# Three passages of a fused decoder layer reordered at once: the last mLSTM head turned sooner, the feed-forward begun under the last memory outputs, a copy and the weight sums moved in the up stage

## Chip, cores and metric

One core of a Trainium2 chip runs the whole kernel. The metric is device time in microseconds (us) from launch to end; lower is better. PE is TensorE, PEld its weight loads, DVE VectorE, ACT ScalarE, POOL GpSimd, SP SyncE, which here only issues DMAs.

## What is computed

A hybrid decoder layer over 1024 positions and 1024 features, f32, batch 1:

```python
h = rmsnorm(x, g_mix)                       # 3360 projected columns: NSA attention and mLSTM heads
x = x + concat(nsa_heads, mlstm_heads) @ w_out          # "mixer output"
q, k, v = rmsnorm(x) @ w_mem_q, rmsnorm(mem) @ w_mem_k, rmsnorm(mem) @ w_mem_v
x = x + softmax(q k^T / 16) v @ w_mem_o                 # "memory outputs"
hf = rmsnorm(x, g_ffn)
a, b = split(causal_conv3(hf @ w_up))                   # "up stage", 2 x 2816 columns
x = x + (gelu(a) * b) @ w_down                          # "down stage"
out = rmsnorm(x, g_final)
```

## The kernel before

**Products.** Activations lie transposed: 128 features on the partitions, 1024 positions along the row; `k` counts the eight feature blocks (KT = 8), `c` the two halves of 512 positions. Every f32 factor is split into a rounded high part and the rest, `h_hi`/`h_lo` and `w_hi`/`w_lo`, and `product` issues three matmuls of 128x512 per block: high by high, low by high, high by low. A weight tile of 128 output columns is so 8 x 2 x 3 = 48 matmuls. They collect in the eight 512-wide banks of PSUM, the tensor `ps`.

**Weights.** SP loads tiles in program order into two raw slots. POOL splits each (`split_tile`: `w_hi` by a multiplication, L871, then `w_lo` by a subtraction, L874) into two slots that alternate. It may write a slot when PE has begun the tile after the one that used it; a `tag` on one matmul of each tile counts the semaphore `tile_started`. `weights_split` tells PE that a tile is ready.

**Order.** Each engine has its own instruction list, written by hand; engines meet only at counting semaphores. DVE and ACT take banks in the order in which PE fills them (`chunk_done`, `chunk_freed`). So an instruction that waits holds up everything behind it on its engine.

**Mixer output.** The first two of eight output tiles (`mixed(z, c, k0, k1)`, z the tile) are interleaved, since the last head's block k = 7 is late: PE turns that head by eight small transposes (`turn_head(MH - 1)`, L1069), DVE scales it (L2404), ACT makes its high part (L1784), DVE its low part (L2137 through `split_head`), and only then may the products on k = 7 run (`split_ready`). Tile 2's weights take tile 0's slot.

**Memory outputs and the start of the feed-forward.** The first two of eight output tiles are interleaved with the attention; a loop (`gemm_loop`) does the other six, tile by tile. DVE adds each tile to the residual `x_t` (L2544, `add_residual`), ACT squares it (L1792) and saves it to DRAM, DVE adds the squares into `acc` (L2149). After the last tile ACT makes 16 high pieces (`split_hi`, L1799) and DVE 16 low pieces (`split_low`, L2138) of `x_t` in `h_hi`/`h_lo`, each a block k of a half c, over the activations that the memory outputs read. The first up tile takes them piece by piece (`plain_tile(0, 0, each_piece)`); behind it PE sums `acc` over features (`token_sums`, L1080), from which the norm's scale comes.

**Up stage.** 22 pairs of tiles p. The first three (PLAIN = 3) are plain; from p = 3 on each pair is one Strassen-Winograd step of seven half-size products of 12 matmuls, in the order a11, s1, s2, a12, s4, a22, s3. ACT makes the high operands and copies two product banks out (`take`, L1933: `p1_sum`, for which a12 waits, and `p5_sum`, for which s4 waits); POOL makes the low operands and sums (L933, L939). At p = 3 ACT first copies the activation operand t3 into `h_hi` (two `t_high`, L1922). In spare places POOL adds pairs of down-projection tiles (`s_new`, L959, "weight sums"): `S_AT` lists for each of the 22 the step at which it is done, two a step in steps 4 to 8 and one a step in 9 to 20. Before each of them SP loads its two tiles, the first two when `t_split` reaches 8, that is when t3's low part is made.

## Time and profile before

| | us |
|---|---|
| median of 3 runs (lowest, highest) | 1771.0 (1769.8, 1777.15) |
| the profiled execution's own time | 1772.6 |
| its span, first to last instruction | 1770.9 |
| PE busy in the span | 1691.8 (96%) |
| DVE / POOL / ACT busy | 1230.1 / 875.5 / 730.0 |
| mean granted TensorE clock | 0.98 of full |

In the timeline a row is: start, duration, engine, line, operation, out<-in, count, and in brackets how long the engine stood idle before it and what ended that. Lines are those of the kernel before. A matmul's duration overlaps the next one's; what counts is the distance between starts.

### The profile page before, as it was taken

What the parts mean: (1) busy time and instruction counts of PE and PEld (TensorE: products, weight loads), DVE (VectorE), ACT (ScalarE), POOL (GpSimd) and SP (SyncE); (2) the same over time, 40 slices, a digit from 0 to 9 for tenths busy, and PEclk for the clock granted to TensorE, in tenths of its full rate; (3) what the DMA queues carried; (4) which work ended last, traced back from release to release, by engine and by line L of the source; (5) the groups of instructions that cost most, each with busy time, mean ns of one, the idle gap of its engine ahead of it and who ended that gap; (6) DMA issues with size and microseconds to landing.
All of it is one profiled execution on the core that took longest, in us unless ns stands there. A gap on an engine that the chain in (4) does not pass through costs nothing.

```text
span 1770.9 us, 23263 instructions
## 1 busy us (share of the span) xinstructions
PE 1691.8 (96%) x8496; PEld 1414.8 (80%) x8496; DVE 1230.1 (69%) x1654; ACT 730.0 (41%) x1367; POOL 875.5 (49%) x671
## 2 busy tenths in 40 slices
PE   7998899999999999899999998989999999999997
PEld 6886788877788888789888776877788888877886
DVE  6754678776777787346554535768887887789965
ACT  5104677876223224115322303434434444543444
POOL 3343344543423332230322443469978878689851
PEclk9998999999999999999999999999999999999999
DMA  5230010110110112224201142145444445685332
GB/s 193 78 120 17 25 37 25 37 37 13 48 48 25 60 48 108 84 95 158 81 25 36 40 151 83 39 140 185 164 139 139 147 136 170 218 314 179 120 130 95
DMA packets 80331, 176.47 MB, mean 100 GB/s; under 512 B 7836, under 2 KB 24412, under 8 KB 80096
## 3 DMA queue, kind: packets, MB, share of 16 engines
q1 hardware_dynamic: 67944, 135.71, 23.2%
q10 hardware_dynamic: 12280, 39.34, 5.9%
q8 instruction: 66, 1.08, 0.3%
q14 instruction: 41, 0.34, 0.1%
HBM read 136.21 MB, written 38.81 MB: 99 GB/s over the span
## 4 chain that ended last, share of the span: by engine, by line
PE 56%; DVE 16%; POOL 11%; ACT 8%; issue 7%; DMA 1%; ACTq 0%; SPq 0%; POOLq 0%; DVEq 0%
PE ps L1028 13%; PE ps L1031 13%; PE ps L1032 13%; DVE x_t L2693 4%; PE ps L1207 3%; ACT x_t L1964 2%; POOL sum_s L939 2%; PE ps L1284 2%; POOL w_lo L933 2%; PE ps L1178 2%; POOL w_lo L989 2%; DVE x_t L2722 2%; PE ps L1226 2%; PE ps L1227 1%; PE ps L1179 1%
## 5 line engine op out<-in xcount | busy, mean ns | idle before, releaser
L1028 PE MATMUL ps<-h_hi,w_hi 128*128 128x512 f32 x1108 | 440.4, 398 | 22.0 <-DVE h_lo L2138 6.0
L1031 PE MATMUL ps<-h_lo,w_hi 128*128 128x512 f32 x1108 | 436.1, 394 | 0.0
L1032 PE MATMUL ps<-h_hi,w_lo 128*128 128x512 f32 x1108 | 435.7, 393 | 0.0
L871 POOL TENSOR_TENSOR w_hi<-w_raw,ones 128x1024 fp32r<-128x1024 f32 x55 | 115.0, 2091 | 549.2 <-PE ps L1028 465.8
L1028 PEld LDWEIGHTS ps<-h_hi,w_hi 128*128 128x128 f32 x1108 | 210.8, 190 | 75.3 <-ACT p_sum L1933 8.4
L1032 PEld LDWEIGHTS ps<-h_hi,w_lo 128*128 128x128 f32 x1108 | 210.7, 190 | 44.7
L1031 PEld LDWEIGHTS ps<-h_lo,w_hi 128*128 128x128 f32 x1108 | 210.9, 190 | 41.8
L899 POOL TENSOR_SCALAR probs<-probs,nsa_inv,gate_sig 128x640 f32<-128x640 f32 (+7 forms) x128 | 100.3, 783 | 172.5 <-DVE nsa_inv L2341 172.5
L2693 DVE SCALAR_TENSOR_TENSOR x_t<-ps,par,x_t 128x1023 f32<-128x1023 f32 x84 | 107.7, 1282 | 79.7 <-ACT x_t L1964 78.2
L874 POOL TENSOR_TENSOR w_lo<-w_raw,w_hi 128x1024 fp32r<-128x1024 f32 x55 | 146.4, 2662 | 4.3
L2137 DVE TENSOR_TENSOR pt_lo<-ps,pt_hi 128x512 fp32r<-128x512 f32 (+1 forms) x148 | 101.8, 688 | 58.0 <-ACT pt_hi L1704 56.1
L1207 PE MATMUL ps<-ident,probs 128*128 128x128 f32 (+1 forms) x592 | 96.4, 288 | 12.2 <-POOL probs L899 6.6
L1704 ACT ACTIVATE pt_hi<-ps 128x512 fp32r<-128x512 f32 (+1 forms) x148 | 87.7, 596 | 45.8 <-PE ps L1207 44.9
L1684 ACT ACTIVATE probs<-ps,nsa_shift 128x640 f32<-128x640 f32 (+7 forms) x128 | 89.8, 702 | 38.5 <-DVE nsa_shift L2329 21.4
L2329 DVE TENSOR_REDUCE nsa_shift<-ps 128x1 f32<-128x640 f32 (+7 forms) x128 | 88.9, 698 | 16.1 <-PE ps L1187 11.1
L1207 PEld LDWEIGHTS ps<-ident,probs 128*128 128x128 f32 (+1 forms) x592 | 65.5, 141 | 25.3 <-DVE pt_lo L2137 11.1
L1178 PE MATMUL ps<-k_a,q_st 128*128 128x512 f32 (+3 forms) x192 | 71.3, 371 | 11.9 <-ACT probs L1684 7.3
L2544 DVE TENSOR_TENSOR x_t<-ps,x_t 128x1024 f32<-128x1024 f32 x16 | 19.5, 1224 | 85.0 <-PE ps L1032 84.9
L2137 DVE TENSOR_TENSOR z_lo<-h_part,z_hi 128x512 fp32r<-128x512 f32 x40 | 58.8, 1484 | 11.7 <-ACT z_hi L2011 11.7
L933 POOL TENSOR_TENSOR w_lo<-w_raw,w_hi 128x512 fp32r<-128x512 f32 x38 | 51.4, 1353 | 29.3 <-ACT w_hi L1951 29.3
L1179 PE MATMUL ps<-k_a,q_st 128*128 128x512 f32 (+3 forms) x192 | 65.6, 348 | 0.0
L1226 PE MATMUL ps<-pt_hi,v_hl 128*128 128x512 f32 x132 | 64.5, 489 | 0.0
(374 smaller groups left out, 4108.5 us busy)
## 6 DMA issues: line engine op xcount, KB each, us to landing
w_raw<-in_w_tiles SPq DMA_DIRECT2D x109, 512.0 KB, 3.4
w_raw<-in_w_tiles SPq DMA_DIRECT2D x55, 256.0 KB, 3.0
s_new<-in_w_tiles SPq DMA_DIRECT2D x44, 256.0 KB, 4.1
z_dram<-x_t ACTq DMA_DIRECT2D x21, 512.0 KB, 2.9
b<-z_dram SPq DMA_DIRECT2D x33, 256.0 KB, 3.9
q_st<-q_dram SPq DMA_DIRECT2D x64, 128.0 KB, 2.8
x_dram<-x_t ACTq DMA_DIRECT2D x14, 512.0 KB, 2.7
t_dram<-t_new ACTq DMA_DIRECT2D x22, 256.0 KB, 5.2
```

Source lines behind the costliest of these rows:

```text
L871: pool.tensor_tensor(w_hi[s][:, :], w_raw[s][:, :], ones[:, :].to_broadcast([P, KT * P]), ALU.mult).then_inc(w_hi_made.sem, w_hi_made.up())
L874: pool.tensor_tensor(w_lo[s][:, :], w_raw[s][:, :], w_hi[s][:, :].bitcast(FP32), ALU.subtract).then_inc(weights_split.sem, weights_split.up())
L899: ins = pool.tensor_scalar(row, row, nsa_inv[:, j % 8, br:br + 1], gate_sig[:, i, 3 * h + 1 + br:3 * h + 2 + br], ALU.mult, ALU.mult)
L1028: ins = mm(out_ap, whi, x_hi, start=first, stop=False)
L1031: mm(out_ap, whi, x_lo, start=False, stop=False)
L1032: return mm(out_ap, wlo, x_hi, start=False, stop=last)
L1178: mm(o, qa, k_a[br][:, g, at_key:at_key + m], start=True, stop=False)
L1207: last = transpose(ps[0:width, 4 + k % 2, hd * P:hd * P + P], probs[:, at_p:at_p + width], ident[:, :])
L1226: mm(o, v, pt_hi[k % 3][0:e, :], start=br == 0 and a == 0, stop=False)
L1684: ins = f(probs[:, P_AT[j]:P_AT[j] + n], flat[:, 0:n], ACT.Exp, bias=nsa_shift[:, j % 8, br:br + 1], accum_out=nsa_sums[:, j % 8, br:br + 1])
L2137: return tt(out_lo, src, hi.bitcast(FP32), ALU.subtract)
L2693: ins = stt(fc[p][i][:, k:SEQ], ps_flat[:, b:b + SEQ - k], conv_f[:, FTAPS - 1 - k, n:n + 1], fc[p][i][:, k:SEQ], ALU.mult, ALU.add)
```

## The change

Three passages change.

1. *Mixer output.* Block k = 7 of tile 0 moves ahead of tile 1's last blocks, the head is turned after the first 12 instead of the first 33 matmuls of tile 1, and the tag that frees tile 0's weight slot sits on the first matmul behind tile 0.
2. *Feed-forward begun under the last memory outputs.* The last two output tiles leave the loop and are interleaved by blocks over banks 4 to 7. `out_read` tells ACT when blocks 0 to 3, and then 4 to 6, have been read, so that pieces (`FRONT`) are written over them while PE still works. The squares of the last two residual blocks come behind the pieces. The first up tile's weights get places of their own (`first_hi`, `first_lo`), split ahead of time.
3. *Up stage.* ACT's two t3 copies move behind the `p1_sum` copy and a tap; the weight sums begin at step 5, two a step in steps 5 to 10 and one a step in 11 to 20.

Two semaphores for small early loads become one (`small_loaded`).

```diff
-S_AT = [p for p in range(PLAIN + 1, FT - 1) for _ in range(2 if p < PLAIN + 6 else 1)]
+S_AT = [p for p in range(PLAIN + 2, FT - 1) for _ in range(2 if p < PLAIN + 8 else 1)]
+FRONT = ([(c, k) for c in range(2) for k in range(4)] + [(0, 4), (0, 5), (0, 6), (0, 7)] + [(1, k) for k in range(4, KT)])
@@ POOL
-            split_pairs((F1 - FIRST_KV - 2 * KT) // 2 - KT // 2 - 1)
+            split_pairs(KT // 2 - 1)
+            pool.wait_ge(loaded[1].sem, loaded[1].next())
+            pool.tensor_tensor(first_hi[:, :], w_raw[1][:, :], ones[:, :].to_broadcast([P, KT * P]), ALU.mult).then_inc(
+                w_hi_made.sem, w_hi_made.up())
+            pool.wait_ge(w_hi_made.sem, w_hi_made.value())
+            pool.tensor_tensor(first_lo[:, :], w_raw[1][:, :], first_hi[:, :].bitcast(FP32), ALU.subtract).then_inc(
+                weights_split.sem, weights_split.up())
+            tile_started.add(1)
+            split_tile(0)
+            split_pairs((F1 - UP) // 2 - 1)
@@ PE, mixer output
-            for z in range(2):
-                first_two.append(next_weights())
-                for c in range(2):
-                    mixed(z, c, 0, 4)
-                for c in range(2):
-                    mixed(z, c, 4, KT - 1)
-                    if z == 1 and c == 0:
-                        turn_head(MH - 1)
-            for z in range(2):
-                for c in range(2):
-                    mixed(z, c, KT - 1, KT).then_inc(chunk_done.sem, chunk_done.up())
+            first_two.append(next_weights())
+            for k0, k1 in ((0, 4), (4, KT - 1)):
+                for c in range(2):
+                    mixed(0, c, k0, k1)
+            first_two.append(next_weights())
+            mixed(1, 0, 0, 4)
+            turn_head(MH - 1)
+            mixed(1, 1, 0, 4)
+            mixed(1, 0, 4, KT - 1)
+            for c in range(2):
+                mixed(0, c, KT - 1, KT).then_inc(chunk_done.sem, chunk_done.up())
+            mixed(1, 1, 4, KT - 1)
+            for c in range(2):
+                mixed(1, c, KT - 1, KT).then_inc(chunk_done.sem, chunk_done.up())
@@ PE, memory outputs
-            gemm_loop(KT // 2 - 1, 2, h_hi, h_lo)
-            freed_now()
+            gemm_loop(KT // 2 - 2, 2, h_hi, h_lo)
+            middle = chunk_done.n
+            ring.resize(4, 4)
...
+            for k0, k1 in ((0, 4), (4, KT - 1)):
+                for z in range(2):
+                    if not k0:
+                        last_two.append(next_weights())
+                    for c in range(2):
+                        ins = last_outputs(z, c, k0, k1)
+                ins.then_inc(out_read.sem, out_read.up())
+            for z in range(2):
+                for c in range(2):
+                    last_outputs(z, c, KT - 1, KT).then_inc(chunk_done.sem, chunk_done.up())
+            taken(middle)
...
-            plain_tile(0, 0, each_piece)
+            plain_tile(0, 0, front_piece, weights=(first_hi, first_lo))
+            h_ready.n = front_from + 2 * KT
+            freed_now()
@@ ACT, memory outputs
+            for n, (c, k) in enumerate(FRONT):
+                if n == 0:
+                    act.wait_ge(t("out_read").sem, 1)
+                elif k == 4 and c == 0:
+                    act.wait_ge(t("out_read").sem, 2)
+                elif k >= KT - 2 and c == 0:
+                    chunk_done.add(2)
+                    freed_now()
+                split_hi(x_t, c * KT + k, c * KT + k + 1, G_FFN)
+            square_and_save(KT - 2)
+            square_and_save(KT - 1)
@@ ACT, up stage
-                if p == PLAIN and PLAIN < FT:
-                    after_product(PLAIN - 1, 7)
-                    for name, part in T_SPLITS[6:]:
-                        t_high(name, part)
                 if PLAIN <= p < FT:
                     take(p, 1, p1_sum, 0, t("p1_taken"))
                 high_operand(p + 1, "a11")
...
                     first_tap(p - 1, 1)
+                if p == PLAIN:
+                    for name, part in T_SPLITS[6:]:
+                        t_high(name, part)
@@ DVE, memory outputs
+            for c, k in FRONT:
+                if c == 0 and k >= KT - 2:
+                    add_output(k)
+                dve.wait_ge(chunk_freed.sem, chunk_freed.value())
+                split_low(x_t, c * KT + k, c * KT + k + 1, G_FFN)
+            for u in range(2):
+                add_square(u)
```

DVE's list at the end of the memory outputs (`x_t<-ps,x_t` is a residual block, `acc<-acc,sq` its squares, `h_lo` a low piece), before:

```order
1064 L2544 TENSOR_TENSOR x_t<-ps,x_t 128x1024 [waits chunk_done,xh_loaded]
1065 L2544 TENSOR_TENSOR x_t<-ps,x_t 128x1024 [waits chunk_done,x_parked]
1066 L2149 TENSOR_TENSOR acc<-acc,sq_167 128x1024 [waits sq_used,sq_ready]
1067 L2149 TENSOR_TENSOR acc<-acc,sq_168 128x1024 [waits sq_used,sq_ready]
1068 L2138 SCALAR_TENSOR_TENSOR h_lo<-x_t,par,h_hi 128x512 [waits hi_ready,chunk_freed]
1069 L2138 SCALAR_TENSOR_TENSOR h_lo<-x_t,par,h_hi 128x512 [waits hi_ready] x15
```

and of the change:

```order
1064 L2195 SCALAR_TENSOR_TENSOR h_lo<-x_t,par,h_hi 128x512 [waits hi_ready,chunk_freed] x10
1065 L2601 TENSOR_TENSOR x_t<-ps,x_t 128x1024 [waits chunk_done,xh_loaded]
1066 L2195 SCALAR_TENSOR_TENSOR h_lo<-x_t,par,h_hi 128x512 [waits hi_ready,chunk_freed]
1067 L2601 TENSOR_TENSOR x_t<-ps,x_t 128x1024 [waits chunk_done,x_parked]
1068 L2195 SCALAR_TENSOR_TENSOR h_lo<-x_t,par,h_hi 128x512 [waits hi_ready,chunk_freed] x5
1069 L2206 TENSOR_TENSOR acc<-acc,sq_167 128x1024 [waits sq_used,sq_ready]
1070 L2206 TENSOR_TENSOR acc<-acc,sq_168 128x1024 [waits sq_used,sq_ready]
```

Ten pieces now stand ahead of the last two residual blocks, and the squares behind all sixteen.

ACT's list around p = 3 of the up stage (`w_hi<-sum_s` is the high part of s3, `h_hi<-x_t` the t3 copy, the first `p_sum` the take for a12, the second the take for s4), before:

```order
701 L1951 ACTIVATE w_hi_53<-sum_s_190 128x512 [waits sum_made]
702 L1922 ACTIVATE h_hi<-x_t 128x2x512 [waits t_made,prod_done]
703 L1922 ACTIVATE h_hi<-x_t 128x2x512 [waits t_made]
704 L1933 ACTIVATE p_sum<-ps 128x512 [waits prod_done]
705 L1951 ACTIVATE spare_hi_181<-w_raw_169 128x512 [waits w_loaded2,prod_done]
706 L1964 ACTIVATE x_t<-ps,par 128x1024 [waits up_ready,z_stored0]
707 L1933 ACTIVATE p_sum<-ps 128x512 [waits prod_done]
```

and of the change:

```order
706 L2009 ACTIVATE w_hi_53<-sum_s_190 128x512 [waits sum_made]
707 L1991 ACTIVATE p_sum<-ps 128x512 [waits prod_done]
708 L2009 ACTIVATE spare_hi_181<-w_raw_169 128x512 [waits w_loaded2,prod_done]
709 L2022 ACTIVATE x_t<-ps,par 128x1024 [waits up_ready,z_stored0]
710 L1980 ACTIVATE h_hi<-x_t 128x2x512 [waits t_made] x2
711 L1991 ACTIVATE p_sum<-ps 128x512 [waits prod_done]
```

The two copies have moved from ahead of the first take to directly ahead of the second.

POOL's list behind the loop that splits the memory output tiles (numbers behind names are buffers), of the change; before, the loop simply ran on over these tiles with `w_hi` and `w_lo`:

```order
219 L929 TENSOR_TENSOR first_hi<-w_raw_52,ones 128x1024 [waits w_loaded1]
220 L932 TENSOR_TENSOR first_lo<-w_raw_52,first_hi 128x1024 [waits w_hi_made]
221 L874 TENSOR_TENSOR w_hi_53<-w_raw_51,ones 128x1024 [waits tile_started,w_loaded0]
222 L877 TENSOR_TENSOR w_lo_55<-w_raw_51,w_hi_53 128x1024 [waits w_hi_made]
223 L285 UNCONDITIONAL_BRANCH
```

The first up tile's split no longer waits for PE to begin a tile; the second one's does, as before.

## Rows read from the trace of the kernel before

**Rows 1.** The page, busy time and instructions of each engine.

```profile
PE 1691.8 (96%) x8496; PEld 1414.8 (80%) x8496; DVE 1230.1 (69%) x1654; ACT 730.0 (41%) x1367; POOL 875.5 (49%) x671
```

**Rows 2.** Timeline of PE, first two mixer output tiles.

```profile
699.79 0.48 PE L1028 MATMUL ps<-h_hi,w_hi 128*128 128x512 f32 x1
...
716.94 1.03 PE L1069 MATMUL ps<-ident,h_mls 128*128 128x128 f32 x8
...
721.82 0.50 PE L1028 MATMUL ps<-h_hi,w_hi 128*128 128x512 f32 x1 [1.79 <-DVE h_lo L2137]
...
728.48 0.79 PE L1028 MATMUL ps<-h_hi,w_hi 128*128 128x512 f32 x1 [3.64 <-POOL w_lo L874]
```

**Rows 3.** Timeline of DVE, then POOL, same stretch.

```profile
708.91 1.23 DVE L2492 TENSOR_TENSOR h_mls<-u_conv,head_d 128x1024 f32<-128x1024 f32 x1
718.07 1.28 DVE L2404 SCALAR_TENSOR_TENSOR o_gate<-ps,par,o_gate 128x1024 f32<-128x1024 f32 x1 [7.93 <-PE ps L1069]
720.54 1.22 DVE L2137 TENSOR_TENSOR h_lo<-o_gate,h_hi 128x1024 fp32r<-128x1024 f32 x1 [1.19 <-ACT h_hi L1784]
...
723.79 1.89 POOL L871 TENSOR_TENSOR w_hi<-w_raw,ones 128x1024 fp32r<-128x1024 f32 x1 [18.98 <-PE ps L1028]
725.76 2.67 POOL L874 TENSOR_TENSOR w_lo<-w_raw,w_hi 128x1024 fp32r<-128x1024 f32 x1
```

**Rows 4.** Windows behind three idle times: from:to, length, busy (matmuls), clock ("PEclk" follows POOL).

```profile
1092.21:1096.56 4.35, 4.34 (x10) 3.46 (x11) 4.35 (x4) 4.35 (x8) 3.42 (x2) 0.51 0.00 0
728.40:734.90 6.50, 6.42 (x16) 5.03 (x17) 6.14 (x6) 2.11 (x2) 4.31 (x3) 0.52 0.25 81
1196.00:1199.00 3.00, 2.94 (x7) 2.39 (x8) 2.69 (x3) 0.85 (x3) 3.00 (x3) 0.52 0.82 210
```

**Rows 5.** Timeline of PE, last two memory output tiles to the token sums.

```profile
1065.66 0.39 PE L1028 MATMUL ps<-h_hi,w_hi 128*128 128x512 f32 x1
...
1092.21 0.77 PE L1028 MATMUL ps<-h_hi,w_hi 128*128 128x512 f32 x1 [4.63 <-DVE h_lo L2138]
...
1106.84 1.84 PE L1080 MATMUL ps<-ones,acc 128*128 128x1 f32 x16
```

**Rows 6.** Timeline of POOL, DVE and ACT, same stretch.

```profile
1068.11 3.26 POOL L874 TENSOR_TENSOR w_lo<-w_raw,w_hi 128x1024 fp32r<-128x1024 f32 x1
...
1087.72 1.22 DVE L2544 TENSOR_TENSOR x_t<-ps,x_t 128x1024 f32<-128x1024 f32 x1 [9.65 <-PE ps L1032]
1088.86 2.54 DVE L2149 TENSOR_TENSOR acc<-acc,sq 128x1024 f32<-128x1024 f32 x2
...
1089.94 9.90 ACT L1799 ACTIVATE h_hi<-x_t,par 128x512 fp32r<-128x512 f32 x16
```

**Rows 7.** Windows of DVE's `h_lo` pieces: from:to, length, busy (pieces), clock.

```profile
1093.00:1098.00 5.00, 5.00 (x3) 0.65 0.00 0
1098.00:1105.80 7.80, 7.77 (x12) 1.00 0.19 67
```

**Rows 8.** Timeline of ACT, PE and POOL, steps 3 and 4 of the up stage.

```profile
1173.78 1.99 ACT L1922 ACTIVATE h_hi<-x_t 128x1024 fp32r<-128x1024 f32 x2
...
1177.66 0.59 ACT L1933 ACTIVATE p_sum<-ps 128x512 f32<-128x512 f32 x1
...
1176.30 0.50 PE L1028 MATMUL ps<-h_hi,w_hi 128*128 128x512 f32 x1 [3.07 <-ACT p_sum L1933]
...
1196.06 0.77 PE L1028 MATMUL ps<-t_hi,spare_hi 128*128 128x512 f32 x1 [2.77 <-POOL spare_lo L933]
...
1201.02 0.50 PE L1028 MATMUL ps<-h_hi,w_hi 128*128 128x512 f32 x1 [0.63 <-ACT p_sum L1933]
...
1188.34 1.30 POOL L959 TENSOR_TENSOR s_new<-s_new,s_new 128x512 f32<-128x512 f32 x1 [5.26 <-DMA s_new<-in_w_tiles]
```

**Rows 9.** Windows: three steps of two weight sums, ten of one; columns as rows 4, POOL fifth.

```profile
1220.53:1279.01 58.48, 58.41 (x253) 46.88 (x253) 49.00 (x46) 24.73 (x37) 54.98 (x40) 1.00 0.48 166
1301.00:1491.50 190.50, 190.50 (x840) 157.13 (x840) 153.52 (x151) 82.43 (x120) 156.76 (x121) 1.00 0.45 149
```

More of the change, by code:

```diff
@@ L489, in build @@
         y_tok = [at(f"y_tok{i}", (32 + 4 * i) * KB, [P, D]) for i in range(TT)]
+        first_hi = at("first_hi", FREE + 96 * KB, [P, KT * P], FP32R)
+        first_lo = at("first_lo", FREE + 100 * KB, [P, KT * P], FP32R)
         part = lambda name, offset, dt=FP32: at(name, offset, [P, HALF], dt)
@@ L2647, in _, with add_output @@
             clear_sums(acc)
-            for n in range(0, KT, 2):
-                for k in (n, n + 1):
-                    if k >= PARK:
-                        back = (t("xh_loaded", 16), t("x_parked", 16))[k % 2]
-                        dve.wait_ge(back.sem, back.next())
-                    add_residual(k)
+            def add_output(k):
+                if k >= PARK:
+                    back = (t("xh_loaded", 16), t("x_parked", 16))[k % 2]
+                    dve.wait_ge(back.sem, back.next())
+                add_residual(k)
+            for n in range(0, KT - 2, 2):
+                add_output(n)
+                add_output(n + 1)
                 for u in range(2):
                     add_square(u)
-            dve.wait_ge(chunk_freed.sem, chunk_freed.value())
-            split_low(x_t, 0, 2 * KT, G_FFN)
+            ring.resize(4, 4)
+            for c, k in FRONT:
[5 more added lines that the diff above has]
+                add_square(u)
             columns_start(4)
```

48 lines of the change are left out of this document (31 added, 17 removed).

## The prediction

> **What bounds the kernel now.** I read the page's busy times first: PE is busy 1691.8 us of 1770.9 [rows 1], so a microsecond counts only if it takes idle or slow time from PE. Then PE's timeline around the three passages. In the mixer output PE stands idle 1.79 us for the last head's block and 3.64 us for a weight tile [rows 2]. Between memory outputs and feed-forward it is idle 4.63 us [rows 5]. In the up stage it waits 3.07, 2.77 and 0.63 us in steps 3 and 4 [rows 8]. Behind three of these idle times the granted clock is 0.51 or 0.52 of full, that is the 1.2 GHz level: 10, 16 and 7 matmuls [rows 4]. At full clock a matmul takes 190.50/840 = 0.2268 us [rows 9], so the slow stretches lose 4.35 - 2.27 = 2.1, 6.5 - 3.6 = 2.9 and 3.0 - 1.6 = 1.4 us.
>
> I make the sum against the profiled execution, 1770.9 us span and 1772.6 us time; that time lies 1.6 us over the median of the three runs, so a saving is taken off 1771.0.
>
> **Mixer output.** The products stay 84, only their order changes. From the start at 699.79, 54 matmuls (42 of tile 0, 12 of tile 1) end at 712.1; there the head is turned, where before it was at 716.94 [rows 2]. Its input is ready at 708.91 + 1.23 = 710.1 [rows 3], so 2.0 us of slack cover this. Before, the low part ended 721.76 - 716.94 = 4.8 us after the turn began [rows 3]; now that is 716.9. The turn costs PE 1.05 us (from 716.94 to 721.82 - 1.79 = 720.03, less 9 matmuls, 2.04), and 21 matmuls (4.8 us) behind it don't need the block: until 717.9. The 1.79 us wait goes, with 1.0 us to spare.
>
> The weight slot: the tag now fires after 6 more matmuls, at 719.3. Before it was the seventh of the last 12, at 723.3, and POOL began at 723.79 and ended 723.79 + 1.97 + 2.67 = 728.43 [rows 3]. Now it begins at 719.8 and ends at 724.4, or 725.0 if its `w_lo` takes the 3.26 us that one takes beside DVE's adds [rows 6]. PE is done with its 15 remaining matmuls at 722.7 and waits 1.7 us, not 3.64. Tile 2 begins at 724.4 instead of 728.48: 4.1 us. Whether the clock falls again adds 2.9 or nothing. The 1.79 us wait was followed by matmuls 0.23 us apart up to the next stop, the 3.64 us one by clock 0.52 [rows 2, 4]; 1.7 us is nearest to the first, so I take full clock: 7.0 us. Ends: 3.5 (slow again, long `w_lo`) and 8.3 (1.79 + 3.64 + 2.9, all gone).
>
> **Start of the feed-forward.** Call 1065.66, where the last two output tiles begin, T. The token sums begin at 1106.84 = T + 41.2 [rows 5]. Between them lie 96 + 48 matmuls, 32.7 us. So at most 8.5 us can go. What waits remain?
>
> First, the second tile's weights are wanted after 24 matmuls (T + 5.4) and not after 48. POOL's `w_lo` begun at 1068.11 ends at 1071.37 = T + 5.7 [rows 6]: a new wait of 0.3 us.
>
> Second, the pieces. Blocks 0 to 3 are read at T + 11.2; their 8 pieces cost ACT 9.90/16 = 0.62 us each [rows 6] and DVE 7.77/12 = 0.65 each [rows 7], and are through by T + 18, four microseconds ahead of PE. Blocks 4 to 6 are read at T + 19.7. Then in a row: ACT 0.6, DVE's pieces (0,4), (0,5) to T + 21.7, the residual block 6 (1.22 [rows 6]) to T + 22.9, ACT 0.8, piece (0,6) to T + 24.4, residual block 7 to 25.6, ACT 0.8, piece (0,7) to T + 27.1. PE ends the outputs at T + 22.1 and has 21 matmuls before block 7: T + 26.9. Alone this waits 0.2 us. But POOL splits the second up tile's weights just then, from PE's start at T + 22.1 on (two instructions, about 2.0 and 2.7 us [rows 3]), and beside such a split DVE got only 3 pieces into 5.00 us where it otherwise did 12 in 7.77 [rows 7]. So a piece gets in between POOL's two instructions, and (0,6) and (0,7) are each about half an instruction late: I take 1.2 us of wait. Then the second half needs no wait: its four late pieces come 0.65 to 1.2 us apart, while 12 matmuls on ready blocks (2.7 us) pass first. The squares follow at T + 31.5 and cost DVE 2.54 [rows 6]: T + 34.1. PE reaches the token sums at T + 32.7 + 0.3 + 1.2 = T + 34.2. Gain 41.2 - 34.2 = 7.0 us. The cover is thin: each microsecond by which DVE is later comes off. Ends: 8.2 (no wait but the first) and 4.8, if both pieces miss POOL's gap and stand behind a whole instruction each (3.4 us of wait). `first_hi`/`first_lo` cost nothing: POOL does them from T + 5.7 to about T + 10.4, 12 us before they are used.
>
> The Trainium skill, "SBUF — State Buffer", section "Who interferes with whom", says that a VectorE instruction with two SBUF inputs and a GpSimd one that reads SBUF can't run together, and that whoever starts first holds the port for the whole instruction. The rows above agree (3 pieces in 5.00 us beside POOL). By the rule alone, with POOL always first, this passage would give the 4.8 us; by the rows 7.0.
>
> **Up stage.** ACT is free at 1173.78, now takes `p1_sum` at once, and a12 begins at 1174.4 instead of 1176.30. But the two copies (1.99 us) now lie ahead of the second take, which ended at 1177.66 + 0.59 = 1178.25 before [rows 8] and ends there still. So s4 begins at 1178.3 after a new wait of 1.2 us; before it began 12 matmuls after 1176.30, at 1179.0. Of 1.9 us only 0.7 stay.
>
> In step 4 POOL's two sums are gone, and with them its 5.26 us wait for their load [rows 8], which came late because the load waits for t3's low part. POOL's next low part then comes over 4 us sooner, before PE asks for it. From s4 at 1178.3 to a12 of step 4 are 6 products, 72 matmuls, 16.3 us: 1194.6, plus 0.2 for the take. Before it was 1201.02 [rows 8]: 6.2 us. This contains the 2.77 us wait and the 1.4 us of slow matmuls.
>
> Against it: a step with two sums lasts 58.48/3 = 19.49 us, one with a single sum 84 x 0.2268 = 19.05 [rows 9]; POOL is busy 54.98 of 58.48 us in the former. Step 4's own two are off the path now, but steps 9 and 10 become double: 2 x 0.44 = 0.9 us back. Net 5.3 us. Ends: 3.3 (2.8 + 1.4 - 0.9, the takes gain nothing) and 7.9 (3.07 + 2.77 + 0.63 + 1.4, no double cost).
>
> The merged semaphore for small loads costs nothing: PE merely waits for one more load of the kernel's first microseconds, over 100 us old by then.
>
> **Sum.** 7.0 + 7.0 + 5.3 = 19.3 us; 1771.0 - 19.3 = 1751.7. The stages behind are PE-bound (190.50 busy of 190.50 [rows 9]), so what is gained stays.
>
> **Rivals.** (a) *Passages half delivered*: clock down behind the 1.7 us wait, pieces behind whole POOL instructions, the takes gaining nothing: 3.5 + 4.8 + 3.3 = 11.6 us, 1759. For it: the port rows; the clock fell after 2.77 and 3.64 us [rows 4, 8]. Against: three independent misfortunes.
> (b) *Given back at the next wait*: the head's low part comes 3.5 us beyond its slack, the squares keep PE from the token sums for as long, and the clock falls at both (2.9 and 2.1 us). The mixer then keeps 7.0 - 6.4 = 0.6 us, the feed-forward 7.0 - 5.6 = 1.4; with 5.3 that is 7.3 us: 1764. For: squares end 0.1 us before they are wanted. Against: nothing in DVE's list grew.
> (c) *Slower*: POOL stalls for the sums' loads in each double step, as at 1188.34, since the sums keep their loads behind the same gate and SP's list is reshuffled. One such stall costs 2.77 + 1.4 = 4.1 us; six of them 24.8, and 19.3 off: 1776.5. It decides from the fifth on. Against: in steps 5 to 8 before, POOL shows no such wait (three double steps are 54.98 of 58.48 busy [rows 9]).
> (d) *All waits go*: 24.4 us, 1747.
>
> **Chances.** Forecast 0.70 (its own range 1748 to 1756), (a) 0.13, (b) 0.08, (c) 0.04, (d) 0.05. The ends of the three terms sum to 11.6 and 24.4 us, so 1746.6 to 1759.4; I give 1747 to 1760. A measurement of this kernel tells 0.5%, some 9 us: faster is forecast, (a) and (d), 0.88; same (b), 0.08; slower (c), 0.04.
>
> **What would show it.** Mixer: turn near 712, no wait on `h_lo` behind it, a wait of 1.4 to 2.3 us on `w_lo`, clock 1.0 behind it. Feed-forward: token sums 34 to 35 us after the last two tiles begin, a wait near 0.3 us on the second tile's weights and one of 0.2 to 3.4 us before block 7 of the first half. Up stage: about 1.2 us between a12 and s4 of step 3, no stall of POOL on `s_new` in step 5, 19.5 us steps from 5 to 10 and 19.05 behind. The prediction is wrong if PE's waits in these places sum to over 8 us, or if a new slow stretch stands behind the 1.7 us wait.

## The result, and the profile after

| | before | after |
|---|---|---|
| median of 4 runs each, taken together | 1770.4 us | 1753.16 us |
| lowest to highest | 1768.93 to 1777.15 | 1752.93 to 1756.01 |
| span of the profiled execution | 1770.9 | 1751.2 |
| mean granted clock | 0.98 | 0.984 |

The ratio is 0.9898, with a 95% interval of 0.9879 to 0.9917: about 18 us faster, between 14.7 and 21.4. The whole interval lies beyond the 0.5% that the prediction named as the bound of a measurement, so this is faster. Predicted were 1751.7 us (1747 to 1760) and 19.3 us of gain.

The page of the changed kernel, busy times. PE's work is the same as in [rows 1], and it lost 5.8 us of busy time; fewer of its matmuls ran at the lower clock (mean granted clock 0.984 instead of 0.98):

```profile
PE 1686.0 (96%) x8496; PEld 1410.7 (81%) x8496; DVE 1231.1 (70%) x1654; ACT 730.7 (42%) x1367; POOL 880.8 (50%) x671
```

**Mixer output.** PE's timeline, changed kernel (start, duration; idle before it and what ended that in brackets), the rows that answer to [rows 2]:

```profile
702.25 0.48 PE L1040 MATMUL ps<-h_hi,w_hi 128*128 128x512 f32 x1
...
714.63 0.38 PE L1081 MATMUL ps<-ident,h_mls 128*128 128x128 f32 x2
...
726.82 0.50 PE L1040 MATMUL ps<-h_hi,w_hi 128*128 128x512 f32 x1 [1.62 <-POOL w_lo L877]
```

DVE and POOL in the same stretch, for [rows 3]:

```profile
715.76 1.28 DVE L2461 SCALAR_TENSOR_TENSOR o_gate<-ps,par,o_gate 128x1024 f32<-128x1024 f32 x1 [3.17 <-PE ps L1081]
718.24 1.23 DVE L2194 TENSOR_TENSOR h_lo<-o_gate,h_hi 128x1024 fp32r<-128x1024 f32 x1 [1.20 <-ACT h_hi L1830]
...
722.10 1.90 POOL L874 TENSOR_TENSOR w_hi<-w_raw,ones 128x1024 fp32r<-128x1024 f32 x1 [14.86 <-PE ps L1040]
724.08 2.69 POOL L877 TENSOR_TENSOR w_lo<-w_raw,w_hi 128x1024 fp32r<-128x1024 f32 x1
```

(The row of the turn shows the first two of its eight transposes.) The head is turned 12.4 us after the start instead of 17.2, no wait for its low part is left, and one of 1.62 us stands before tile 2. Tile 2 begins 24.57 us after the start (726.82 - 702.25) instead of 28.69.

**Start of the feed-forward.** PE's timeline, for [rows 5]:

```profile
1058.28 0.39 PE L1040 MATMUL ps<-h_hi,w_hi 128*128 128x512 f32 x1
...
1064.04 0.50 PE L1040 MATMUL ps<-h_hi,w_hi 128*128 128x512 f32 x1 [0.16 <-POOL w_lo L877]
...
1086.34 0.50 PE L1040 MATMUL ps<-h_hi,first_hi 128*128 128x512 f32 x1 [0.91 <-DVE h_lo L2195]
...
1092.59 1.84 PE L1092 MATMUL ps<-ones,acc 128*128 128x1 f32 x16
```

The last two output tiles begin at 1058.28, the token sums 34.3 us later instead of 41.2. DVE and POOL there, for [rows 6]:

```profile
1080.14 1.22 DVE L2601 TENSOR_TENSOR x_t<-ps,x_t 128x1024 f32<-128x1024 f32 x1
1082.22 1.26 DVE L2195 SCALAR_TENSOR_TENSOR h_lo<-x_t,par,h_hi 128x512 fp32r<-128x512 f32 x1 [0.86 <-ACT h_hi L1845]
1083.41 1.21 DVE L2601 TENSOR_TENSOR x_t<-ps,x_t 128x1024 f32<-128x1024 f32 x1
...
1088.86 2.54 DVE L2206 TENSOR_TENSOR acc<-acc,sq 128x1024 f32<-128x1024 f32 x2
...
1081.04 1.90 POOL L874 TENSOR_TENSOR w_hi<-w_raw,ones 128x1024 fp32r<-128x1024 f32 x1 [11.75 <-PE ps L1040]
1083.02 2.72 POOL L877 TENSOR_TENSOR w_lo<-w_raw,w_hi 128x1024 fp32r<-128x1024 f32 x1
```

The piece (0,6) at 1082.22 lasts 1.26 us, twice a piece's usual time. It begins while POOL's `w_hi` runs and ends 0.54 us after that has ended. The squares end at 1091.4, 1.2 us before the token sums.

**Up stage.** PE, then ACT, for [rows 8]:

```profile
1150.66 0.39 PE L1040 MATMUL ps<-h_hi,spare_hi 128*128 128x512 f32 x1
...
1160.16 0.50 PE L1040 MATMUL ps<-h_hi,w_hi 128*128 128x512 f32 x1 [1.18 <-ACT p_sum L1991]
...
1164.07 0.50 PE L1040 MATMUL ps<-h_hi,w_hi 128*128 128x512 f32 x1 [0.87 <-ACT p_sum L1991]
...
1180.93 0.50 PE L1040 MATMUL ps<-h_hi,w_hi 128*128 128x512 f32 x1 [0.25 <-ACT p_sum L1991]
...
1161.54 1.99 ACT L1980 ACTIVATE h_hi<-x_t 128x1024 fp32r<-128x1024 f32 x2
1163.43 0.59 ACT L1991 ACTIVATE p_sum<-ps 128x512 f32<-128x512 f32 x1
```

From a11 of step 3 to a12 of step 4 (1150.66 to 1180.93) PE takes 30.27 us instead of 36.11. The second wait is the one predicted behind the two copies.

The clock, in windows of the changed kernel (from:to, length, busy of PE, PEld, DVE, ACT, POOL, granted clock, DMA share, GB/s): behind tile 2's wait, behind the take for a12, and three double steps, for [rows 4, 9]:

```profile
726.80:733.30 6.50, 6.48 (x28) 5.36 (x29) 6.08 (x7) 2.13 (x2) 4.31 (x2) 1.00 0.31 94
...
1160.10:1163.10 3.00, 2.94 (x12) 2.17 (x12) 1.39 (x2) 3.00 (x5) 3.00 (x3) 1.00 0.34 98
1199.91:1258.40 58.49, 58.47 (x254) 46.79 (x253) 48.99 (x46) 24.73 (x37) 55.04 (x39) 1.00 0.51 176
```

Where the 19.7 us between the spans lie, by landmarks in PE's timeline:

| stretch | before | after | gain |
|---|---|---|---|
| start to the mixer output | 699.79 | 702.25 | -2.5 |
| to tile 2 | 28.69 | 24.57 | 4.1 |
| to the last two memory output tiles | 337.2 | 331.5 | 5.7 |
| to the token sums | 41.2 | 34.3 | 6.9 |
| to a11 of step 3 | 58.07 | 58.07 | 0 |
| to a12 of step 4 | 36.11 | 30.27 | 5.8 |
| to the down stage's first product (1538.07, 1518.84) | 337.05 | 337.91 | -0.9 |
| to the end | 232.8 | 232.4 | 0.5 |

### The profile page after: what moved, and what is told of

It reads as the page before. It is cut to its first block, busy times and chain, and to the rows that moved or that the text cites. A ratio compares the mean times of both kernels' runs of the same rounds, so it can differ in the third digit from the quotient of the medians.

```text
span 1751.2 us, 23264 instructions
## 1 busy us (share of the span) xinstructions
PE 1686.0 (96%) x8496; PEld 1410.7 (81%) x8496; DVE 1231.1 (70%) x1654; ACT 730.7 (42%) x1367; POOL 880.8 (50%) x671
## 4 chain that ended last, share of the span: by engine, by line
PE 54%; DVE 14%; POOL 13%; issue 9%; ACT 8%; DMA 1%; SPq 0%; ACTq 0%; POOLq 0%; DVEq 0%
PE ps L1040 13%; PE ps L1044 12%; PE ps L1043 12%; DVE x_t L2760 4%; PE ps L1219 3%; POOL sum_s L951 2%; ACT x_t L2022 2%; PE ps L1296 2%; POOL w_lo L945 2%; PE ps L1190 2%; PE ps L1238 2%; POOL w_lo L1001 2%; DVE x_t L2789 1%; PE ps L1191 1%; PE ps L1239 1%
## 5 line engine op out<-in xcount | busy, mean ns | idle before, releaser
L1040 PE MATMUL ps<-h_hi,w_hi 128*128 128x512 f32 x1092 | 430.2, 394 | 12.0 <-POOL w_lo L877 5.4
L1044 PE MATMUL ps<-h_hi,w_lo 128*128 128x512 f32 x1092 | 425.8, 390 | 0.0
L1043 PE MATMUL ps<-h_lo,w_hi 128*128 128x512 f32 x1092 | 425.7, 390 | 0.0
L1040 PEld LDWEIGHTS ps<-h_hi,w_hi 128*128 128x128 f32 x1092 | 205.3, 188 | 63.1 <-ACT p_sum L1991 8.0
L1044 PEld LDWEIGHTS ps<-h_hi,w_lo 128*128 128x128 f32 x1092 | 205.2, 188 | 43.4
L1043 PEld LDWEIGHTS ps<-h_lo,w_hi 128*128 128x128 f32 x1092 | 205.5, 188 | 41.2
```

What stands on the lines that cost most here:

```text
L1040: ins = mm(out_ap, whi, x_hi, start=first, stop=False)
L1043: mm(out_ap, whi, x_lo, start=False, stop=False)
L1044: return mm(out_ap, wlo, x_hi, start=False, stop=last)
```

## Experiments

Ratios are against the kernel before on the same chip, each with its 95% interval. Many distances between landmarks of PE's timeline repeat to 0.1 us from run to run and are the sharper measure. That does not hold where a slow stretch comes and goes, nor where a chain waits for a load: such distances differ by 1 us and more with the same code, and each is known here from one profiled execution of a kernel.

**One passage at a time.** The first three are the kernel before with one passage of the change, its hunks as shown above: PE's order, turn and tag in the mixer output (`e1_mixer`); the last two tiles, the pieces and `first_hi`/`first_lo` (`e2_front`); `S_AT` and the copies (`e3_up`). `e2_front` also has the merged semaphore `small_loaded`, the other three don't. The fourth takes one line of the third:

```diff
-S_AT = [p for p in range(PLAIN + 1, FT - 1) for _ in range(2 if p < PLAIN + 6 else 1)]
+S_AT = [p for p in range(PLAIN + 2, FT - 1) for _ in range(2 if p < PLAIN + 8 else 1)]
```

> The kernel before with the first passage alone (mixer output), nothing else changed. My theory: the head is turned some 12.4 us after the first product of the mixer output, no wait for its low part, a wait of about 1.6 us on the third tile's low weights in place of 1.79 and 3.64, so tile 2 begins 4.1 us sooner after the mixer's start, and 2.9 us more come from the clock that no longer falls behind the wait: 7.0 us in all, 1763.6 against 1770.4, ratio 0.996. If the clock falls all the same: 4.1 us, 0.9977. If the gain is given back at the next wait of the memory outputs (the head start is lost before their last two tiles): under 1 us, with tile 2 sooner but the token sums as far from the mixer's start as before, 404 to 407 us.

> The kernel before with the second passage alone (last two memory output tiles interleaved, pieces by blocks, places of their own for the first up tile's weights). My theory: from the start of the last two tiles to the token sums 34.3 us in place of 41.2, with waits of 0.2 us for the second tile's weights and 0.9 us before block 7 of the first half: 6.9 us, about 1763.5, ratio 0.996. If the gain is given back at a later wait (the up stage's first Strassen step needs ACT and POOL at a fixed distance from the squares' end): the distance from the token sums to the a11 product of step 3 grows from 58.07 us, and the ratio is above 0.998.

> The kernel before with the third passage alone (t3 copies behind the take for a12, weight sums from step 5 on). My theory: 6 us between the a11 product of step 3 and the a12 product of step 4 (36.1 to 30.2), less 0.8 for two more steps with two weight sums: 5.1 to 5.3 us, about 1765.2, ratio 0.997. If the two added double steps cost more than I read from the steps of before (1.5 us each in place of 0.44), 3 us, 0.9983. If POOL stalls on the loads of the sums: steps 5 to 10 longer than 19.5 us and the ratio at 1 or above.

> The kernel before with one line of the third passage, the list that places the weight sums one step later (no sum at step 4); the t3 copies stay ahead of the take for a12. My theory: the two later waits of that stretch (2.77 us and 0.63 us before the products of step 4, and the slow clock between them) come from the sum at step 4, which waited 5.26 us for its load; they go, the wait of 3.07 us for the take does not: about 3.4 to 3.9 us between the a11 product of step 3 and the a12 product of step 4, less 0.8 for the double steps, so 2.6 to 3.1 us, ratio 0.9983, and the copies make up the other 2 to 2.5 of the passage. Rival: the sum is nearly all of it (the wait for the take is answered by a later one anyway): 4.5 us or more, 0.9975. Second rival, the copies are nearly all of it: under 1 us.

| kernel | ratio | its landmarks |
|---|---|---|
| mixer output alone | 0.9951 [0.9934, 0.9967] | start to tile 2 24.58 us, wait 1.62, full clock behind |
| feed-forward alone | 0.9955 [0.9939, 0.9970] | wait before block 7 0.91; tile 2 still 28.65 with the slow stretch |
| up stage alone | 0.9964 [0.9952, 0.9976] | a11 of step 3 to a12 of step 4 30.24; behind it 337.70 |
| weight sums alone | 0.9981 [0.9969, 0.9994] | the same 32.19; behind it 337.63 |

Each passage gives its part alone. The windows behind tile 2's wait show the clock term, mixer output alone and then feed-forward alone:

```profile
723.90:730.40 6.50, 6.41 (x28) 5.34 (x29) 6.08 (x7) 2.13 (x2) 4.34 (x3) 1.00 0.27 89
```

```profile
727.90:734.30 6.40, 6.37 (x15) 5.03 (x16) 6.08 (x6) 2.11 (x2) 4.28 (x2) 0.51 0.22 82
```

28 matmuls against 15 in about the same time. From tile 2 to the next landmark (the transposes of `xv_feat`) PE needs 116.3 us in the first and 119.2 in the second: 2.9 us. From a wait of 2.05 us at a fixed place of the memory outputs to the token sums it is 78.02 us with the feed-forward passage and 84.86 to 84.88 in the three kernels without it: 6.8 us (before it is 86.42, with a stretch of 7 matmuls at half the clock in it that those three don't have). The sums alone shorten the up stage's stretch by 36.11 - 32.19 = 3.9 us; the copies make up the other 1.95. So the cause of most of that passage is the sum in step 4. Its 3.9 us is the value of one execution, since what it costs depends on when its two loads land: POOL waits 5.26 and 1.18 us for them before, and 4.72 and 0.74 us in the kernel with the mixer output passage alone, whose up stage is the same, and there the stretch is 35.13 us, which makes the sum worth 2.9. The three ratios add to 23 us (8.7, 8.0, 6.4), each uncertain by 2 to 3. The landmarks add to 19.0 (7.0, 6.8, 5.2). The whole change has 7.0, 6.9 and 5.0 at the same places, if the clock term of 2.9 is taken from the passage alone.

**The port: POOL's split out of DVE's way.** The changed kernel with

```diff
             tile_started.add(1)
+            pool.wait_ge(t("h_ready").sem, 4 * KT + 4)
             split_tile(0)
```

> The changed kernel, except that POOL begins to split the second up tile only when ACT has made all sixteen pieces (a wait on the pieces' count ahead of that split). Theory: the two instructions of that split (1.90 and 2.72 us) lie over DVE's residual blocks and low pieces and slow them; with them out of the way the wait of 0.91 us before block 7 of the first half falls to 0.2 us or less, and the token sums come 0.7 us sooner after the last two tiles begin (33.6 in place of 34.3). Rival: that wait is the chain from the last product of tile 6 through DVE's addition, ACT and DVE alone, and stays at 0.8 to 1.0 us; the time is the same within 0.2 us. Either way the second up tile must still be ready when the first ends (12 us later), or a new wait stands there.

The count that POOL waits for is that of DVE's low pieces (the expectation says ACT's): its split begins at 1090.39, right behind the last of the sixteen.

Ratio 0.9894 [0.9877, 0.9911], no different from the change. PE, then DVE and POOL (product lines are here L1041 to L1045):

```profile
1087.71 0.50 PE L1041 MATMUL ps<-h_hi,first_hi 128*128 128x512 f32 x1 [0.35 <-DVE h_lo L2196]
...
1094.44 1.92 PE L1093 MATMUL ps<-ones,acc 128*128 128x1 f32 x16 [0.28 <-DVE acc L2207]
1096.55 0.50 PE L1041 MATMUL ps<-h_hi,w_hi 128*128 128x512 f32 x1 [0.19 <-POOL w_lo L877]
...
1098.07 0.63 PE L1045 MATMUL ps<-h_hi,w_lo 128*128 128x512 f32 x1
...
1090.24 4.06 DVE L2207 TENSOR_TENSOR acc<-acc,sq 128x1024 f32<-128x1024 f32 x2
...
1090.39 2.83 POOL L874 TENSOR_TENSOR w_hi<-w_raw,ones 128x1024 fp32r<-128x1024 f32 x1 [19.15 <-DVE h_lo L2196]
```

The wait before block 7 fell from 0.91 to 0.35, so 0.56 us of it was POOL's split. The other 0.35 us stays, more than the 0.2 or less that was expected. But the split now lies over the squares: 4.06 us where they took 2.54, and POOL's own instruction 2.83 instead of 1.90. Two small waits take the first one's place, and the clock falls behind them (matmuls of 0.63): from the token sums to a11 of step 3 it is 60.1 us, not 58.07. The token sums come 34.20 us after the last two tiles begin, where 33.6 was expected and the change has 34.32. So the theory had one cause of the wait right, and was wrong on the time.

**The copies once more.** The changed kernel with the two t3 copies behind the second take:

```diff
-                if p == PLAIN:
-                    for name, part in T_SPLITS[6:]:
-                        t_high(name, part)
...
                     take(p, 2, p5_sum, 1, t("p5_taken"))
+                if p == PLAIN:
+                    for name, part in T_SPLITS[6:]:
+                        t_high(name, part)
```

> The changed kernel, except that ACT makes the two t3 copies of step 3 behind the take for s4 instead of ahead of it. Theory: the wait of 0.87 us before s4 is those two copies (1.99 us each) ahead of the take on ACT; it goes, and nothing takes its place, since t3 is read only by the last product of the step: a11 of step 3 to a12 of step 4 29.4 us in place of 30.3. Rival: DVE's low part of t3 (4.05 us) begins later by as much, s3 of step 3 or POOL's sum loads behind it wait, and the distance stays at 30.3 or grows.

Ratio 0.9898 [0.9880, 0.9916]. PE of this kernel:

```profile
1157.43 0.50 PE L1040 MATMUL ps<-h_hi,w_hi 128*128 128x512 f32 x1 [1.18 <-ACT p_sum L1991]
...
1178.23 0.50 PE L1040 MATMUL ps<-h_hi,w_hi 128*128 128x512 f32 x1 [0.84 <-ACT p_sum L1991]
```

The wait of 0.87 us before s4 went (the two copies take 1.99 us together, not each, as the expectation has it), and 20.80 us after a12 of step 3 PE waits 0.84 for a12 of step 4, where the change had 20.77 and a wait of 0.25. So the gain is given back in full, as the rival said, but by another chain than the rival's. In the changed kernel a chain, at each link of which one engine goes on as soon as the one before it has ended, runs from ACT's tap at 1160.53 to that take at 1180.30:

```profile
1161.67 2.60 DVE L2760 SCALAR_TENSOR_TENSOR x_t<-ps,par,x_t 128x1023 f32<-128x1023 f32 x2 [2.52 <-ACT x_t L2022]
1164.19 4.05 DVE L2194 TENSOR_TENSOR h_lo<-x_t,h_hi 128x1024 fp32r<-128x1024 f32 x2
...
1169.60 1.22 DVE L2789 TENSOR_TENSOR x_t<-x_t 128x1024 f32<-128x1024 f32 x1
...
1171.23 0.63 ACT L2009 ACTIVATE w_hi<-w_raw 128x512 fp32r<-128x512 f32 x1 [5.63 <-DVE x_t L2789]
...
1174.51 0.64 ACT L2009 ACTIVATE w_hi<-sum_s 128x512 fp32r<-128x512 f32 x1 [2.65 <-POOL sum_s L951]
```

With DVE's low part of t3 (4.05 us) in it, this chain of DVE, ACT and POOL ends after PE does, whatever PE waited for before. From the tap to the take it is 19.8 us in both kernels. The run with the weight sums alone has it too: the copies stand ahead of the first take there, PE doesn't wait before s4 and runs 8 matmuls at half the clock behind a12 of step 3, and a12 of step 4 follows 20.80 us later all the same.

**What a double step costs.** The changed kernel with eleven double steps:

```diff
-S_AT = [p for p in range(PLAIN + 2, FT - 1) for _ in range(2 if p < PLAIN + 8 else 1)]
+S_AT = [p for p in range(PLAIN + 2, PLAIN + 13) for _ in range(2)]
```

> The changed kernel with the 22 weight sums two a step in steps 5 to 15 and none behind, in place of two in 5 to 10 and one in 11 to 20. Same work, eleven double steps in place of six. What a double step costs is what I took 0.9 us from (0.44 each, by the steps' lengths 19.5 and 19.05). If that price belongs to the double step and a step with no sum gains nothing over a step with one: 5 x 0.44 = 2.2 us slower. If the price is proportional to the number of sums (each costs what it costs, wherever it stands): no difference, 0.0 to 0.3 us. If it belongs to the loads that then come faster: over 3 us.

Ratio 0.9892 [0.9874, 0.9909]. The eleven double steps, and five with no sum:

```profile
1198.75:1413.15 214.40, 214.28 (x926) 172.16 (x926) 178.85 (x166) 91.23 (x134) 198.84 (x143) 1.00 0.50 171
1413.15:1508.35 95.20, 95.20 (x422) 78.86 (x421) 75.97 (x77) 42.16 (x61) 70.24 (x55) 1.00 0.37 122
```

214.40/11 = 19.49 and 95.20/5 = 19.04 us: a step with no sum is no shorter than one with a single sum, and the price of 0.44 belongs to the double step. From a12 of step 4 to the down stage it is 339.81 us instead of 337.91, 1.9 more. But from there to the end it is 230.7 instead of 232.4, so that most of it comes back. That was not expected. What differs at the start of the down stage is that SP issued the two loads of the residual 0.2 us after its first product and not 3.0.

**Tag and turn of the mixer output, one at a time.** The changed kernel, once with the tag that frees tile 0's weight slot put back on block 7 of tile 1's first half, where the kernel before has it (the expectation says the second half's), and once with the turn 12 matmuls later:

```diff
-... tag=(c, k) == ((0, 0), (1, 4))[z])
+... tag=(c, k) == ((0, 0), (0, KT - 1))[z])
```

```diff
-            turn_head(MH - 1)
             mixed(1, 1, 0, 4)
+            turn_head(MH - 1)
```

> The changed kernel with one of the three edits of the first passage taken back: tile 0's weight slot is released by the last block of tile 1 (second of its halves' blocks 7), not by the first matmul behind tile 0. The head is still turned early. Theory: the wait on the third tile's low weights grows from 1.62 to about 4.8 us (the split starts when tile 0's last products are long done but the tag comes some 3.5 us later), the clock falls behind it, and the mixer passage loses 3 us or, with the slow stretch, 6. Rival: POOL's split is late for its own reasons (its own list or the raw load) and the tag does not matter: wait 1.6 us as now.

> The changed kernel with the head turned behind 24 matmuls of tile 1 instead of 12, so that 9 matmuls stand between the turn and its block, as in the kernel before; the tag stays early. Theory: a wait of 1.8 us on the head's low part returns and the one of 1.62 us on the third tile's low weights stays: tile 2 26.4 us after the mixer's start in place of 24.57. On the clock: in all four executions profiled so far with a wait of 1.8 us on the head and then one of 3.6 us the clock was at its lower level behind the second; with the single wait of 3.33 us (late tag) it stayed at full. If the pair of waits in short order does it, a slow stretch returns here (another 2.9 us before the memory stage); if only the length of the second wait counts, none, and the loss is 1.8 us alone.

Late tag: 0.9898 [0.9881, 0.9914]. POOL's `w_hi` begins 21.9 us after the start of the mixer output (722.17 - 700.28) instead of 19.85, PE waits 3.33 us, and tile 2 stands at 26.3 instead of 24.57. The tag is worth 1.7 us. I had put its delay at 3.5 us; it is 2.0, which is the nine matmuls that lie between the two places (9 x 0.2268). The expectation had the clock fall behind the wait and the wait grow to 4.8 us; neither came. Late turn: 0.9913 [0.9891, 0.9935], PE of this kernel and a window between its two waits:

```profile
724.96 0.50 PE L1040 MATMUL ps<-h_hi,w_hi 128*128 128x512 f32 x1 [1.80 <-DVE h_lo L2194]
...
731.97 0.50 PE L1040 MATMUL ps<-h_hi,w_hi 128*128 128x512 f32 x1 [0.32 <-POOL w_lo L877]
...
726.50:729.80 3.30, 3.30 (x9) 2.61 (x8) 2.22 (x3) 0.98 (x3) 2.50 (x2) 0.50 0.00 0
```

The 1.8 us wait returned, and tile 2 stands at 27.0, where 26.4 was expected without a slow stretch. The wait for tile 2's weights shrank to 0.32. The clock was down, as the theory of two waits wanted, but from 1.5 us behind the first wait on, 5 us before the second. So that theory is not confirmed, nor is the one by length: the late tag's wait of 3.33 us had full clock behind it, this one of 1.80 the lower one. What decides stays open.

**Two more moves in PE's order.** In the changed kernel, block 7 of tile 0 and the tag 3 matmuls sooner, and the first up tile's halves interleaved:

```diff
-            mixed(1, 0, 4, KT - 1)
+            mixed(1, 0, 4, KT - 2)
             for c in range(2):
                 mixed(0, c, KT - 1, KT).then_inc(chunk_done.sem, chunk_done.up())
+            mixed(1, 0, KT - 2, KT - 1)
...
+FIRST_ORDER = ([(0, k) for k in range(6)] + [(1, k) for k in range(4)] + [(0, 6), (0, 7)] +
+               [(1, k) for k in range(4, KT)])
```

> The changed kernel with two more moves in PE's order. In the mixer output block 7 of the first tile comes one block (3 matmuls, 0.7 us) sooner, and the tag with it. In the first up tile the two halves are interleaved: blocks 0 to 5 of half 0, 0 to 3 of half 1, then 6 and 7 of half 0, and the rest. My theory: the wait of 1.62 us on the third tile's low weights falls to 0.95 and the distance from the mixer's start to tile 2 from 24.6 to 23.9 us; the wait of 0.91 us before block 7 of half 0 goes, because 12 matmuls (2.7 us) now stand ahead of it, and the token sums come 33.4 us after the last two tiles begin in place of 34.3. Sum 1.6 us, about what repeated executions of one kernel differ by, so it is read from the trace. Rival: a wait of the same size on a later piece or on the head's low part takes its place (the head's chain of 4.9 us from the turn has 18 matmuls, 4.1 us, and the turn's own 0.9 ahead of it: no slack), and the distances stay at 24.6 and 34.3.

Ratio 0.9892 [0.9871, 0.9914], profiled span 1751.4 us. Start to tile 2 fell to 23.98 us with a wait of 0.94; the wait before block 7 is gone, and from the fixed wait in the memory outputs to the token sums it is 76.93 instead of 77.98 us. Both landmarks moved as my theory said, 1.6 us together, and neither wait came back elsewhere. The median does not show it, nor could it: the runs of this kernel differ by 5 us.

**The down stage.** The down stage gave and took 2 us in the run with eleven double steps, so two runs asked why. The first ends the sums at step 19 (changed kernel, seven double steps):

```diff
-S_AT = [p for p in range(PLAIN + 2, FT - 1) for _ in range(2 if p < PLAIN + 8 else 1)]
+S_AT = [p for p in range(PLAIN + 2, FT - 2) for _ in range(2 if p < PLAIN + 9 else 1)]
```

> The changed kernel with seven double steps (5 to 11) and the weight sums ending at step 19 instead of 20. In the run with eleven double steps the up stage was 2.0 us longer, as priced, but the down stage 2 us shorter: SP could load a residual and the weights behind it 2.4 us sooner against the down stage's first product, and the wait of 1.55 us on a low part was gone. Theory: it is the sum of step 20 that puts POOL, then ACT's tap, then DVE's convolution and the store to DRAM behind; without it the down stage is 1.5 to 2 us shorter for 0.44 us more in the up stage, a net of 1 to 1.5 us. Rival: what shortened the down stage there was that no sum ran in the last five steps: then 0.44 us longer, and the down stage as now (232.4 us from its first product to the end).

Ratio 0.9894 [0.9873, 0.9915]. The up stage was 0.6 us longer and the down stage 235.0 us, 2.6 us longer than in the change, with a wait of 3.32 us before its ninth product (the expectations count it as the eleventh). So leaving out the sum of step 20 did not shorten it. More one execution can't tell, since the run with the copies moved once more had 234.7 us in a down stage that its edit doesn't touch. The second starts from the kernel with two more moves and puts the residual's loads later on SP:

```diff
-            for half in range(2):
-                ks = slice(4 * half, 4 * half + 4)
-                sp.dma_start(x_res[:, ks, :], ...)
             for g, (n, k) in enumerate(DOWN_STEPS):
...
+                if g in (10, 13):
+                    half = (10, 13).index(g)
+                    ks = slice(4 * half, 4 * half + 4)
+                    sp.dma_start(x_res[:, ks, :], ...)
```

> The kernel of the run with PE's order changed in two more places, and one move on SP: the two loads of the residual for the down stage (2048 KB each) no longer stand ahead of its first three weight tiles but behind the third of them and three more loads on. In the twelve kernels profiled so far the third of the new weight loads reached ACT 19.0 to 22.6 us after the down stage's first product, and the wait of 0 to 3.3 us before the down stage's eleventh product followed that landing alone: 1.45 us in the run this starts from. Theory: those tiles queue behind the residual, and land several us sooner now; the wait goes, the first addition to the residual (38 us after the down stage's first product) still finds it loaded: the down stage is 1.2 to 1.6 us shorter, 230.7 to 231 us from its first product to the end in place of 232.3. Rival 1: the loads from the stored copies, now behind the residual, arrive late and a wait of the same size stands at a later product. Rival 2: the transfers were not what they waited for (the slot is freed late by POOL): no change.

Ratio 0.9873 [0.9851, 0.9896], median 1750.13 us, the lowest of all kernels here. The wait before the ninth product is gone, as the theory said: the issues of the three weight loads there last 0.4 to 0.6 us each, where in the changed kernel they last up to 1.47. They land 5.2 to 5.9 us after their issue instead of 9.4 to 12.8. And yet the down stage takes 233.7 us, 1.4 more than in the kernel that it starts from. POOL shows why, this kernel and then the changed one:

```profile
1561.50 1.29 POOL L998 TENSOR_TENSOR h_part<-h_part,w_raw 128x512 f32<-128x512 f32 x1 [4.96 <-DMA w_raw<-in_w_tiles]
...
1561.50:1633.00 71.50, 68.66 (x291) 53.27 (x289) 62.91 (x48) 27.15 (x46) 71.50 (x45) 1.00 0.46 157
...
1633.05 0.50 PE L1043 MATMUL ps<-w_hi 128*128 128x512 f32 x1 [0.41 <-POOL w_lo L1004]
```

```profile
1564.03 1.29 POOL L995 TENSOR_TENSOR h_part<-h_part,w_raw 128x512 f32<-128x512 f32 x1 [2.42 <-DMA w_raw<-in_w_tiles]
...
1564.00:1635.60 71.60, 69.94 (x306) 56.45 (x304) 65.40 (x50) 27.36 (x48) 71.57 (x45) 1.00 0.49 161
...
1635.59 0.50 PE L1040 MATMUL ps<-w_hi 128*128 128x512 f32 x1 [0.40 <-POOL w_lo L1001]
```

From the moment at which POOL gets the first weight tile of the second set, some 45 us into the down stage, it is busy 71.5 of 71.5 us, and PE waits for it at the end of that. What PE saved earlier it spends here in small waits. In 12 of the 14 profiled kernels the time from that landing to the end is 187.1 to 187.2 us, in the other two 187.7, while the landing itself lies between 43.6 us after the down stage's first product (eleven double steps) and 47.8 (sums ended at 19). Here it lies at 46.5, where the kernel that this one starts from has 45.1, and that is the 1.4 us. The load was issued nearly as soon (40.5 us after the first product and 40.2), but took 5.9 us to land instead of 4.8. So rival 1 has the right shape, with a load of weights in place of a stored copy. What made it land later stays open. Whether the lower median of this kernel is a gain stays open: its interval overlaps that of the kernel it starts from, and its profiled span is 2.7 us shorter only because its first 699.0 us were 4.9 us shorter, in a part that neither touches.

## Why the prediction was right

**Mixer output, 7.0 us: right.** Turn, wait (1.7 us predicted, 1.62 measured), 4.1 us and full clock came as worked out; the clock term is 2.9 by the passage alone. In all nine profiled kernels with the early turn the clock stayed up behind the wait on `w_lo`, six times of 1.62 us. The reason I gave, likeness to the 1.79 us wait, was a guess that held: in the run with the late turn just such a wait of 1.80 did have the lower clock behind it.

**Feed-forward, 7.0 us: right**, 6.9 and 6.8. The terms were 0.16 for the second tile's weights (0.3 predicted), 0.91 before block 7 (1.2 predicted), no wait for the squares. They ended 1.2 us ahead of the token sums, where I had 0.1. The share of POOL's split in the wait is 0.56 us by experiment. By the rule of the Trainium skill in "SBUF — State Buffer", section "Who interferes with whom", that a VectorE instruction with two SBUF inputs and a GpSimd one that reads SBUF exclude each other, this passage would have given 4.8 us with POOL always first. The traces agree with the rule (squares 4.06 instead of 2.54 us beside a split), but POOL was not always first: the piece got in between POOL's instructions.

**Up stage, 5.3 us: right.** 5.84 measured for 6.2, less 0.86 for 0.9; 5.2 by the passage alone. The wait before s4 was 0.87 for 1.2. One link of the mechanism was missing: I let a12 of step 4 follow s4 after 72 matmuls plus 0.2, and it was in fact held by the chain of DVE, ACT and POOL from the first tap, 20.8 us behind a12 of step 3, which the sixth experiment found. That the number came right all the same is luck: the chain happens to end only 0.25 us after PE. Nor are the 1.4 us of slow matmuls a term of this passage: in the kernel before, PE still waited 0.63 us for the take behind them, so the take and not PE's clock set that landmark.

**The sum.** The three terms are worth 19.0 us by their landmarks. The other parts of the span difference are not the change's: 2.5 us lost before the mixer output, and 2.8 won between tile 2 and the last memory output tiles, beyond the slow stretch. Of the latter, 1.6 us is a slow stretch that stood near 1021.5 before, and 1.2 us lies around a wait of 0.97 at 824.87. Among the 13 other kernels only one has the first. The three without the mixer passage don't have the second, and two with it have one at that place, of 0.41 and 0.84 us. The 2.5 us lost and the 2.8 won nearly cancel, and that the spans differ by 19.7 us, so near the 19.3 predicted, is luck to that extent; the median came 1.5 us above the predicted 1751.7. "What is gained stays" held, but its reason did not: what sets the length of the down stage is a landing 45 us into it and, for 70 us behind that, POOL. It moves with its start, and took 232.3 to 234.7 us in the eleven kernels that don't edit it or the sums behind step 10.

**The rivals.** (a) and (d) did not come. (b), given back at the next wait, did not happen to the change but to three attempts at more: the copies, the port and the residual's loads. (c), stalls of POOL for the sums' loads, did not occur: in none of the eleven kernels whose sums begin at step 5 does POOL wait for a sum's load, and in three double steps of the changed kernel it is busy 55.04 of 58.49 us, as before.

## What to carry to other kernels

Count, for each wait that goes, what else ends just behind it: on this kernel a wait of 0.87 us was worth nothing since a chain of other engines ended 0.25 us after PE, and one of 1.45 us since a load further on landed 1.4 us later and POOL, full for 70 us behind it, could not catch up. The distance between two landmarks that frame an edit can show 0.1 us where the median of runs shows 3. Build the sum from such distances, look in other runs whether they repeat, and check it by running each passage alone. A busy share of PE near 100% in a stretch says that nothing waits there, not that a later stretch starts when this one ends.
